# A two-attention transformer kernel: in the first attention the turn of a finished output moves behind the next tile's values, into the banks of the turned weights

## The chip, the core and the metric

The kernel runs on one core of a Trainium2 chip. The metric is device time in microseconds (us) from the start to the end of one launch. The core has five engines that run their own instruction lists in order and meet at semaphores: TensorE (PE in the rows; its weight loads are PEld), VectorE (DVE), ScalarE (ACT), GpSimd (POOL) and SyncE (SP), which issues most of the transfers. Matrix products and transposes land in PSUM, eight banks of 128 x 512 float32.

## The reference

Two transformer blocks run one after the other on 1024 tokens of width 1024. The change touches only the attention of the first one:

```python
def forgetting_attention(q, k, v, log_f):
    scale = 1.0 / math.sqrt(dh)
    c = jnp.cumsum(log_f, axis=1).transpose(0, 2, 1)
    ...
    def one_block(args):
        q_i, c_i, s0 = args
        scores = jnp.einsum('bqhd,bkhd->bhqk', q_i, k).astype(jnp.float32) * scale
        scores = scores + c_i[:, :, :, None] - c[:, :, None, :]
        ...
        scores = jnp.where(causal, scores, -jnp.inf)
        probs = jax.nn.softmax(scores, axis=-1).astype(v.dtype)
        return jnp.einsum('bhqk,bkhd->bqhd', probs, v)
```

There are 8 heads of width 64 and 8 blocks of 128 queries. Before it stand a norm and the projection, behind it the pooled branch, the output product and the gated feed-forward layer; the second block has two layers, the last of which holds a second attention (`diff_attention`, 6 heads of width 128).

## The kernel before

A class `Attention` serves both attentions; `diff` is true in the second one. The first handles its heads in four pairs (`n` = 4), one behind the other, and in each pair eight tiles of 128 queries (`iq` = 0 to 7), 32 tiles in all. A tile with index `iq` sees `iq` + 1 blocks of 128 keys, so "the five-block tile" below is `iq` = 4. Tile `t` goes through these steps (class, then the line of its main instruction):

- `Scores`: TensorE multiplies queries by keys into banks 0 to 3 (L1760); VectorE adds the bias and takes the maximum, once for each of the two heads (L1778, then L1781).
- `Exponentials`: ScalarE (L1791), once for each head. `Normalise`: VectorE takes the reciprocals of the sums (L1799, L1801).
- `Values`: the weights are turned on TensorE in groups of up to four blocks (L1827) into bank 4 + g % 2, where g is the running number of the group; each group is copied to SBUF and multiplied by the values (L1836) into the output's bank 6 + `iq` % 2. A tile of up to four blocks has two groups, one for each head; a larger one has four: four blocks and the rest of head 0, then the same of head 1.
- `ScaleOut`: VectorE divides the output by the sums (L1870). `TurnOut`: TensorE turns it (L1891), and ScalarE copies it away (L1898).

`Attention.steps` sets the order, which is the same for every engine. For tile t it is: `Normalise`(t), `ScaleOut`(t-1), `Scores`(t+1), `TurnOut`(t-1), all of `Values`(t), `Exponentials`(t+1). `fill` puts nothing in between in the first attention. Inside `Values` the list of TensorE is: turn group 1, turn group 2, multiply group 1, turn group 3, multiply group 2, and so on.

Who copies a turned group depends on its number alone:

```python
    def copied(self, g):
        return "pt_dve" if g % 2 and not self.diff else "pt_act"
```

An even g is copied by ScalarE (L1849), an odd one by VectorE (L1858). Every tile has an even count of groups, and g starts at zero, so group 1 of a tile is always even and ScalarE's. In VectorE's list the copies of tile t stand behind both bias passes of tile t+1. The turned output shares the bank of its own values (6 or 7, columns 128 to 255). `Prepare` and `Join` stand around the attention: no engine goes on before all are done.

Of the kernel before, what the change touches and what calls it, by code (L numbers as in the profile page):

```python
# [1636 lines left out]
class Attention:  # L1637
# [6 lines left out]
    def __init__(self, k, n, q, keys, v, out, sc, pt, on, nkeys, bias, diff=False, out_banks=2, ready=lambda i, iq: ()):  # L1644
        self.k, self.s, self.id = k, k.s, k.new_id()
        self.n, self.q, self.keys, self.v, self.out, self.nkeys, self.bias, self.diff = n, q, keys, v, out, nkeys, bias, diff
        self.out_banks, self.ready, self.waited = out_banks, ready, set()
        self.sc, self.pt, self.on = k.at(sc, 4, S), k.at(pt, 2, HALF), k.at(on, 2, P)
        self.heads = 1 if diff else 2
        self.per_pair = sum(self.of_tile(iq) for iq in range(ST))  # L1650
        self.outs = {self.out_group(i, iq) for i in range(n) for iq in range(ST)} if diff else set()

    def stat(self, iq, h):
        c = 4 * ((2 * iq + h) % 16)
# [5 lines left out]
    def steps(self, fill=lambda t, place: ()):  # L1660


        part = lambda kind, t, *more: [kind(self.k, self, *divmod(t, ST), *more)]
        last = self.n * ST - 1
        out = part(Scores, 0) + part(Exponentials, 0)
        for t in range(last + 1):
            out += part(Normalise, t)
            if t:
                out += part(ScaleOut, t - 1)
            if t < last:  # L1670
                out += part(Scores, t + 1)
            out += fill(t, 0)
            if t and not self.diff:
                out += part(TurnOut, t - 1)
            out += fill(t, 1)
            for n in range(len(self.groups(*divmod(t, ST))) + 1):
                out += part(Values, t, n)
                if n == 0:
                    out += fill(t, 2)
            if t < last:  # L1680
                out += part(Exponentials, t + 1)
            if t and self.diff:
                out += part(TurnOut, t - 1)
            out += fill(t, 3)
        return out + part(ScaleOut, last) + part(TurnOut, last)

    def groups(self, i, iq):


        g = i * self.per_pair + sum(self.of_tile(j) for j in range(iq))  # L1690
        if self.diff:
            g += max(i * ST + iq - 1, 0)
        nj, out = self.nkeys(iq) // P, []
        for h in range(self.heads):
            for first in range(0, nj, 4):
                out.append((g, h, first, min(4, nj - first)))
                g += 1
        return out
# [113 lines left out]
class Values(AttentionStep):  # L1812
# [7 lines left out]
    def pe(self, pe):  # L1820
        k, s, of, i, iq = self.k, self.s, self.of, self.i, self.iq
        for g, h, first, m in self.turned:
            if first == 0:
                pe.wait_ge(*s["combined" if of.diff else "exped"].at((of.id, i, iq, h)))
            k.bank_free(pe, 4 + g % 2)
            for j in range(m):
                ins = pe.transpose(k.ps[:, 4 + g % 2, j * P:(j + 1) * P], of.sc[:, of.buf(iq, h), (first + j) * P:(first + j + 1) * P], k.ident)  # L1827
            ins.then_inc(*s.turned_p.up((of.id, g)))
            k.free[4 + g % 2] = (of.copied(g), (of.id, g))
        for g, h, first, m in self.valued:  # L1830
            nj, b, o = of.nkeys(iq) // P, of.out_bank(iq), slice(0, P) if of.diff else slice(64 * h, 64 * h + 64)
            if first == 0 and h == 0:
                k.bank_free(pe, b)
            pe.wait_ge(*s[of.copied(g)].at((of.id, g)))
            for j in range(m):
                ins = pe.matmul(k.ps[:, b, o], of.pt[:, g % 2, j * P:(j + 1) * P], of.v(i, first + j)[:, o],  # L1836
                                start=(first + j == 0), stop=(first + j == nj - 1))
            ins.then_inc(*s.valued.up((of.id, g)))
            if of.diff:
                k.free[b] = ("scaled_out", (of.id, i, iq))  # L1840

    def act(self, act):
# [8 lines left out]
    def dve(self, dve):  # L1851
        k, s, of = self.k, self.s, self.of
        for g, h, first, m in self.turned:
            if of.copied(g) == "pt_dve":
                dve.wait_ge(*s.turned_p.at((of.id, g)))
                if g > 1:
                    dve.wait_ge(*s.valued.at((of.id, g - 2)))
                dve.tensor_copy(of.pt[:, g % 2, 0:m * P], k.ps[:, 4 + g % 2, 0:m * P]).then_inc(*s.pt_dve.up((of.id, g)))  # L1858


# [13 lines left out]
class TurnOut(AttentionStep):  # L1874


    def place(self):
        k, of = self.k, self.of
        if of.diff:
            b = 4 + of.out_group(self.i, self.iq) % 2  # L1880
            return b, k.ps[:, b, 0:P]
        b = of.out_bank(self.iq)
        return b, k.ps[:, b, P:2 * P]

    def pe(self, pe):
        k, s, of, i, iq = self.k, self.s, self.of, self.i, self.iq
        b, to = self.place()
        pe.wait_ge(*s.scaled_out.at((of.id, i, iq)))
        if of.diff:
            k.bank_free(pe, b)  # L1890
        pe.transpose(to, of.on[:, iq % 2, :], k.ident).then_inc(*s.turned_out.up((of.id, i, iq)))  # L1891
        k.free[b] = ("out_copied", (of.id, i, iq))

# [1431 lines left out]
```

## Time and profile before

| What | us |
|---|---|
| median of 3 runs | 3353.5 |
| the runs | 3343.42, 3353.5, 3353.6 |
| the profiled execution | 3344.59 |
| its span, first to last instruction | 3343.3 |
| TensorE busy in it | 2864.3 (86%) |
| VectorE, ScalarE, GpSimd busy | 1715.0, 986.0, 686.9 |
| first attention, first score to last copy | 254 to 442 |
| second attention | about 2865 to 3162 |

The profiled execution's time is its span and 1.3 us around it. It stands near the lowest of the three runs; the other two are 9 us above it. A busy share says little by itself here: TensorE has the largest one, but inside an attention tile it stops for the other engines several times, and what a change is worth is read from those stops. The column PEclk of the windows is the clock that TensorE was granted: 1.00 is 2.4 GHz and 0.50 is 1.2 GHz.

### The profile page before, as it was taken

The numbers are of one execution on the slowest core, as the hardware profiler recorded it, in microseconds if no ns is written. First come the engines' busy times: TensorE is split into PE (matmuls) and PEld (weight loads), VectorE is DVE, ScalarE is ACT, GpSimd is POOL, SyncE is SP. The second block draws the span as 40 slices with busy tenths as digits, with TensorE's granted clock in tenths as the row PEclk, the third lists the DMA queues.
The fourth block names the chain that finished last, engine by engine and source line by source line (L and its number), as shares of the span: only waits on it lengthen the run. The fifth ranks groups of instructions, "written<-read, shape, count | busy, mean of one in ns | idle before, by whom it ended". The sixth has DMA issues, their size and how long they took to land.

```text
span 3343.3 us, 49988 instructions
## 1 busy us (share of the span) xinstructions
PE 2864.3 (86%) x20746; PEld 2296.5 (69%) x20746; DVE 1715.0 (51%) x3034; ACT 986.0 (29%) x1803; POOL 686.9 (21%) x531
## 2 busy tenths in 40 slices
PE   7978878699999999689999867777748899999767
PEld 6765667588888888567888646666627678766545
DVE  3425555544444444666554157777654433377634
ACT  3224444311111111633221211111143222255543
POOL 2112233211011110262111012222212211122123
PEclk9988999899999999899999968998979899999978
DMA  3111032011111111113112100000032201111222
GB/s 105 45 51 39 14 100 65 26 58 50 45 51 51 45 51 50 39 57 94 45 38 64 55 1 3 3 3 3 3 113 76 92 29 44 34 33 35 79 82 76
DMA packets 196450, 162.46 MB, mean 49 GB/s; under 512 B 5200, under 2 KB 173818, under 8 KB 195458
## 3 DMA queue, kind: packets, MB, share of 16 engines
q1 hardware_dynamic: 196226, 159.26, 15.1%
q8 instruction: 167, 2.74, 0.3%
q14 instruction: 57, 0.47, 0.0%
HBM read 137.19 MB, written 22.05 MB: 48 GB/s over the span
## 4 chain that ended last, share of the span: by engine, by line
PE 70%; DVE 16%; ACT 6%; issue 4%; POOL 2%; DMA 2%; SPq 0%; POOLq 0%; DVEq 0%; ACTq 0%
PE ps L721 15%; PE ps L723 14%; PE ps L722 14%; PE ps L2267 5%; PE ps L1836 3%; PE ps L1760 3%; DVE r L686 2%; PE ps L1462 1%; PE ps L1464 1%; PE ps L1463 1%; PE ps L773 1%; ACT r L681 1%; PE ps L1827 1%; PE ps L775 1%; PE ps L774 1%
## 5 line engine op out<-in xcount | busy, mean ns | idle before, releaser
L721 PE MATMUL ps<-r,r 128*128 128x512 f32 (+1 forms) x2304 | 939.7, 408 | 145.5 <-DVE r L686 118.5
L722 PE MATMUL ps<-r,r 128*128 128x512 f32 (+1 forms) x2304 | 911.1, 395 | 0.0
L723 PE MATMUL ps<-r,r 128*128 128x512 f32 (+1 forms) x2304 | 910.6, 395 | 0.0
L721 PEld LDWEIGHTS ps<-r,r 128*128 128x128 f32 x2304 | 444.6, 193 | 280.7 <-DVE r L686 132.1
L667 POOL TENSOR_TENSOR sb<-sb 128x1024 f32<-128x1024 f32 x138 | 281.6, 2046 | 1350.7 <-DMA sb<-in_w_ffn_up 483.5
L722 PEld LDWEIGHTS ps<-r,r 128*128 128x128 f32 x2304 | 445.3, 193 | 93.2 <-issue 6.2
L723 PEld LDWEIGHTS ps<-r,r 128*128 128x128 f32 x2304 | 443.3, 192 | 94.9
L2267 PE MATMUL ps<-sb 64*64 64x64 f32 (+2 forms) x8832 | 299.6, 226 | 120.0 <-DVE sb L2515 31.4
L2267 PEld LDWEIGHTS ps<-sb 64*64 64x64 f32 (+1 forms) x8832 | 278.9, 135 | 150.4 <-issue 100.1
L686 DVE TENSOR_TENSOR r<-sb,r 128x1024 fp32r<-128x1024 f32 x198 | 273.9, 1391 | 190.9 <-ACT r L681 190.5
L681 ACT CAST r<-sb 128x1024 fp32r<-128x1024 f32 x198 | 204.9, 1043 | 229.0 <-POOL sb L667 228.9
L1836 PE MATMUL ps<-sb 128*128 128x64 f32 (+1 forms) x1008 | 144.2, 288 | 22.2 <-ACT sb L1849 17.2
L1836 PEld LDWEIGHTS ps<-sb 128*128 128x128 f32 x1008 | 131.3, 201 | 41.8 <-issue 20.9
L1462 PE MATMUL ps<-r,r 128*128 128x512 f32 x352 | 138.7, 394 | 8.1 <-DVE sb L1475 7.5
L926 DVE TENSOR_TENSOR sb<-sb 128x512 f32<-128x512 f32 x70 | 61.9, 885 | 163.2 <-ACT sb L916 151.7
L1414 ACT CAST r<-sb 128x512 fp32r<-128x512 f32 x44 | 27.3, 620 | 384.9 <-DVE sb L1429 384.9
L1463 PE MATMUL ps<-r,r 128*128 128x512 f32 x352 | 137.1, 389 | 0.0
L1464 PE MATMUL ps<-r,r 128*128 128x512 f32 x352 | 137.1, 389 | 0.0
L1778 DVE CUSTOM_DVE_ANT_0 sb<-ps,sb 128x128 f32<-128x128 f32 (+7 forms) x160 | 121.0, 756 | 28.0 <-PE ps L1760 20.5
L1475 DVE TENSOR_TENSOR sb<-sb,ps 128x512 f32<-128x512 f32 x160 | 105.9, 684 | 54.6 <-PE ps L1464 54.6
L1791 ACT ACTIVATE sb<-sb 128x128 f32<-128x128 f32 (+7 forms) x160 | 123.1, 772 | 26.3 <-DVE sb L1781 25.8
L1760 PE MATMUL ps<-sb 64*128 64x512 f32 (+2 forms) x480 | 103.6, 537 | 23.7 <-DVEq L298 16.1
(276 smaller groups left out, 3602.1 us busy)
## 6 DMA issues: line engine op xcount, KB each, us to landing
sb<-in_w_out SPq DMA_DIRECT2D x36, 512.0 KB, 4.0
sb<-in_a_w_in SPq DMA_DIRECT2D x29, 512.0 KB, 4.0
sb<-in_w_ffn_gate SPq DMA_DIRECT2D x22, 512.0 KB, 3.8
sb<-in_w_ffn_up SPq DMA_DIRECT2D x22, 512.0 KB, 3.8
sb<-in_w_ffn_down SPq DMA_DIRECT2D x22, 512.0 KB, 3.5
sb<-in_w_in SPq DMA_DIRECT2D x17, 512.0 KB, 4.0
sb<-in_x SPq DMA_DIRECT2D x16, 512.0 KB, 5.5
xs<-sb SPq DMA_DIRECT2D x4, 2048.0 KB, 9.7
```

Source lines behind the costliest of these rows:

```text
L667: pool.tensor_tensor(w.raw, w.raw, w.gain.unsqueeze(2).broadcast_to((P, w.nk, w.n)), ALU.mult).then_inc(*s.w_gain.up(w.id))
L681: act.copy(w.hi, w.raw).then_inc(*s.w_hi.up(w.id))
L686: dve.tensor_tensor(w.lo, w.raw, w.hi.bitcast(F32), ALU.subtract).then_inc(*s.w_lo.up(w.id))
L721: pe.matmul(self.out, w.hi[:, q, self.cols], hi, start=(q == 0), stop=False)
L722: pe.matmul(self.out, w.hi[:, q, self.cols], lo, start=False, stop=False)
L723: ins = pe.matmul(self.out, w.lo[:, q, self.cols], hi, start=False, stop=(q == w.nk - 1))
L1462: pe.matmul(self.out, w.hi[:, 0, cols], hi, start=(q == 0), stop=False)
L1463: pe.matmul(self.out, w.hi[:, 0, cols], lo, start=False, stop=False)
L1464: ins = pe.matmul(self.out, w.lo[:, 0, cols], hi, start=False, stop=(q == 1))
L1760: ins = pe.matmul(k.banks(2 * h)[:, b:b + m], of.q(i)[o, iq * P:(iq + 1) * P], of.keys(i)[o, b:b + m], start=True, stop=True)
L1836: ins = pe.matmul(k.ps[:, b, o], of.pt[:, g % 2, j * P:(j + 1) * P], of.v(i, first + j)[:, o], start=(first + j == 0), stop=(first + j == ...
L2267: ins = pe.matmul(self.bank(b + p // n, n, w)[o, p % n, :], lhs[o, p], rhs[o, p], start=(j == 0), stop=(j == len(pairs) - 1), skip_group_c ...
```

## The change

`TurnOut`(t-1) of the first attention moves behind all of `Values`(t) and `Exponentials`(t+1), where the second attention has had it. Its result now goes into bank 4 or 5, as if it were one more group of turned weights, so it takes a number g of its own, and all later groups move on by one.

```diff
-        self.outs = {self.out_group(i, iq) for i in range(n) for iq in range(ST)} if diff else set()
+        self.outs = {self.out_group(i, iq) for i in range(n) for iq in range(ST)}
...
             out += fill(t, 0)
-            if t and not self.diff:
-                out += part(TurnOut, t - 1)
             out += fill(t, 1)
...
             if t < last:
                 out += part(Exponentials, t + 1)
-            if t and self.diff:
+            if t:
                 out += part(TurnOut, t - 1)
...
-        if self.diff:
-            g += max(i * ST + iq - 1, 0)
+        g += max(i * ST + iq - 1, 0)
...
-            if of.diff:
+            if (g, h, first, m) == self.g[-1]:
                 k.free[b] = ("scaled_out", (of.id, i, iq))
...
-                if g > 1:
-                    dve.wait_ge(*s.valued.at((of.id, g - 2)))
+                if of.pt_before(g) >= 0:
+                    dve.wait_ge(*s.valued.at((of.id, of.pt_before(g))))
...
     def place(self):
-        k, of = self.k, self.of
-        if of.diff:
-            b = 4 + of.out_group(self.i, self.iq) % 2
-            return b, k.ps[:, b, 0:P]
-        b = of.out_bank(self.iq)
-        return b, k.ps[:, b, P:2 * P]
+        b = 4 + self.of.out_group(self.i, self.iq) % 2
+        return b, self.k.ps[:, b, 0:P]
...
         pe.wait_ge(*s.scaled_out.at((of.id, i, iq)))
-        if of.diff:
-            k.bank_free(pe, b)
+        k.bank_free(pe, b)
```

`copied` is unchanged. The file is three lines shorter above the touched classes, so L1760 becomes L1757, L1827 becomes L1824, L1836 becomes L1833, L1858 becomes L1855, L1778 becomes L1775, and L1891 becomes L1883.

TensorE's list at the five-block tile of the second pair: behind the next tile's scores (L1760) stands the turned output, then the turned groups and the products. A row ends in the semaphores that its instruction waits for; `s_pt_act` and `s_pt_dve` are ScalarE's and VectorE's copies of turned weights. Before:

```order
L1760 MATMUL ps<-sb 128x256 x2
L1891 MATMUL ps<-sb 128x128 [waits s_scaled_out]
L1827 MATMUL ps<-sb 128x128 [waits s_pt_act,s_exped]
L1827 MATMUL ps<-sb 128x128 x3
L1827 MATMUL ps<-sb 128x128 [waits s_pt_dve]
L1836 MATMUL ps<-sb 128x64 [waits s_pt_act,s_out_copied]
L1836 MATMUL ps<-sb 128x64 x3
L1827 MATMUL ps<-sb 128x128 [waits s_pt_act,s_exped]
L1827 MATMUL ps<-sb 128x128 x3
L1836 MATMUL ps<-sb 128x64 [waits s_pt_dve]
```

Now:

```order
L1757 MATMUL ps<-sb 128x256 x2
L1824 MATMUL ps<-sb 128x128 [waits s_pt_dve,s_exped]
L1824 MATMUL ps<-sb 128x128 x3
L1824 MATMUL ps<-sb 128x128 [waits s_out_copied]
L1833 MATMUL ps<-sb 128x64 [waits s_pt_dve,s_scaled_out]
L1833 MATMUL ps<-sb 128x64 x3
L1824 MATMUL ps<-sb 128x128 [waits s_pt_dve,s_exped]
L1824 MATMUL ps<-sb 128x128 x3
L1833 MATMUL ps<-sb 128x64 [waits s_pt_act]
```

The turned output has left this place (it stands behind the tile's last product as L1883), and the product of group 1 now waits for VectorE's copy, that of group 2 for ScalarE's.

VectorE's list at the same tile, from the first bias pass of the next tile (768 keys; ISA is the fused add and maximum) to the copies. Before:

```order
L1778 ISA sb<-ps,sb 128x768 [waits s_turned_p,s_bias_made,s_scored]
L1778 ISA sb 128x1
L1781 TENSOR_SCALAR sb<-sb 128x1 [waits s_biased]
L1858 COPY sb<-ps 128x128 [waits s_valued,s_turned_p] x2
L1799 RECIPROCAL sb<-sb 128x1 [waits s_exped]
```

Now:

```order
L1775 ISA sb<-ps,sb 128x768 [waits s_turned_p,s_bias_made,s_scored]
L1775 ISA sb 128x1
L1778 TENSOR_SCALAR sb<-sb 128x1 [waits s_biased]
L1855 COPY sb<-ps 128x512 [waits s_valued,s_turned_p] x2
L1796 RECIPROCAL sb<-sb 128x1 [waits s_exped]
```

VectorE's two copies have grown from 128 to 512 columns, and ScalarE has the two of 128 instead. The place of the copies in the list is the same. It is so in the tiles of one, three, five and seven blocks (but for the very first tile), since one number goes to an output per tile and the numbers of every second tile become odd where they were even; the tiles of two, four, six and eight blocks keep their copies. The lists of GpSimd and SyncE, and everything outside the first attention, are the same.

## Rows read from the trace of the kernel before

**Rows 1.** windows, first attention; us, busy of PE, PEld, DVE, ACT, POOL, PEclk, DMA

```profile
260.48:278.06 17.58, 17.28 (x60) 11.09 (x61) 8.28 (x37) 6.03 (x21) 5.06 (x8) 0.50 0.00 1
278.06:442.12 164.06, 143.72 (x1026) 111.00 (x1024) 94.16 (x327) 77.33 (x186) 35.82 (x52) 1.00 0.05 20
260.48:309.83 49.35, 45.67 (x272) 33.97 (x272) 25.74 (x93) 21.20 (x55) 11.38 (x18) 0.82 0.06 22
356.20:399.98 43.78, 38.46 (x274) 29.43 (x273) 25.72 (x92) 20.98 (x53) 10.63 (x16) 1.00 0.06 25
```

**Rows 2.** timeline, five-block tile, third pair; start, length, engine, line, [idle before]

```profile
369.06 1.56 PE L1760 MATMUL ps<-sb 64*128 64x512 f32 x8
...
370.71 0.71 PE L1827 MATMUL ps<-sb 128*128 128x128 f32 x5
...
372.08 1.08 PE L1836 MATMUL ps<-sb 128*128 128x64 f32 x8 [0.66 <-ACT sb L1849]
...
372.88 0.29 DVE L1858 COPY sb<-ps 128x128 f32<-128x128 f32 x1
...
372.99 0.61 PE L1827 MATMUL ps<-sb 128*128 128x128 f32 x4
...
374.28 1.33 PE L1836 MATMUL ps<-sb 128*128 128x64 f32 x10 [0.39 <-ACT sb L1849]
...
375.53 1.77 PE L1760 MATMUL ps<-sb 64*128 64x512 f32 x8
```

**Rows 3.** timeline, seven-block tile, third pair

```profile
382.45 1.99 PE L1760 MATMUL ps<-sb 64*128 64x512 f32 x8
...
384.53 0.93 PE L1827 MATMUL ps<-sb 128*128 128x128 f32 x7
...
387.23 0.56 DVE L1858 COPY sb<-ps 128x384 f32<-128x384 f32 x1
...
388.89 1.70 PE L1836 MATMUL ps<-sb 128*128 128x64 f32 x14
...
390.52 0.49 PE L1760 MATMUL ps<-sb 64*128 64x128 f32 x4
```

**Rows 4.** timeline, three-block tile, third pair

```profile
362.51 0.56 DVE L1858 COPY sb<-ps 128x384 f32<-128x384 f32 x1
...
363.12 0.88 PE L1836 MATMUL ps<-sb 128*128 128x64 f32 x6 [0.24 <-DVE sb L1858]
...
363.93 1.35 PE L1760 MATMUL ps<-sb 64*128 64x512 f32 x8
```

**Rows 5.** groups of instructions by form, 254 to 482 us; busy, mean ns | idle before

```profile
L1898 ACT COPY sb<-ps 128x128 f32<-128x128 f32 x32 | 8.5, 266 | 65.6 <-PE ps L1891 65.6
...
L1858 DVE COPY sb<-ps 128x512 f32<-128x512 f32 x12 | 8.3, 692 | 12.3 <-PE ps L1827 12.3
...
L1891 PEld LDWEIGHTS ps<-sb 128*128 128x128 f32 x32 | 4.6, 143 | 17.5 <-DVE sb L1870 14.1 <-issue 3.1
```

**Rows 6.** windows, second attention: six stops of TensorE and the 3.0 us after each

```profile
2935.44:2940.96 5.52, 2.67 (x23) 2.46 (x23) 4.42 (x12) 3.17 (x9) 3.75 (x2) 1.00 0.00 0
2979.35:2984.87 5.52, 3.00 (x14) 2.72 (x14) 4.25 (x11) 2.96 (x9) 3.99 (x3) 0.69 0.15 45
3025.77:3031.29 5.52, 2.72 (x15) 2.47 (x16) 4.41 (x12) 3.17 (x9) 3.74 (x2) 0.81 0.00 0
3071.04:3076.56 5.52, 3.00 (x14) 2.72 (x14) 4.25 (x11) 2.95 (x9) 3.99 (x3) 0.73 0.14 43
3113.54:3118.84 5.30, 2.67 (x22) 2.46 (x23) 3.98 (x14) 2.47 (x9) 0.00 (x0) 1.00 0.00 0
3154.20:3159.93 5.73, 2.68 (x19) 2.47 (x19) 1.93 (x4) 2.12 (x5) 0.00 (x0) 0.91 0.02 4
```

**Rows 7.** timeline, TensorE alone, first pair

```profile
268.72 2.08 PE L1760 MATMUL ps<-sb 64*128 64x512 f32 x4
...
275.23 2.51 PE L1760 MATMUL ps<-sb 64*128 64x512 f32 x8
```

## The prediction

> **What bounds the kernel now.** The change lives in the first attention, so I read the windows of that stretch first [rows 1]. From 278 us on TensorE is granted the full clock, 2.4 GHz (1.00), and is busy for 143.72 of 164.06 us; a pair of heads takes 43.78 us there and repeats to the hundredth. TensorE is the bound, with stops. In the first 17.58 us it runs at 1.2 GHz (0.50), and the first pair takes 49.35 us for the same work. Then the timeline of single tiles shows what ends the stops. At the five-block tile [rows 2] TensorE does the next tile's scores from 369.06, turns groups 1 and 2 from 370.71, and multiplies group 1 at 372.08, as soon as ScalarE has copied it. VectorE, meanwhile, does the two bias passes of the next tile; only at 372.88 is it free for its copy of group 2, and TensorE is then still busy with group 1. So the slow copier sits where it is covered: behind a group that ScalarE delivers early. The three-block tile shows the same end without enough cover: VectorE copies at 362.51, and TensorE has waited 0.24 us when it multiplies at 363.12 [rows 4].
>
> **Part 1, the turn leaves its place.** Its weight load waits 17.5 us in all, most of it for the scaling on VectorE, and ScalarE's 32 copies of it (266 ns each, 8.5 us) stand ahead of the first copy of turned weights [rows 5]. That wait is gone: groups 1 and 2 are turned earlier by the turn's own share of the list, between 0.11 us (the step from one transpose to the next) and 0.28 (one alone) [rows 2]; I take 0.16. But nearly nothing follows, since the next wait in the tile is for VectorE's copy, which stands behind the bias passes, and those start at the end of the scores, which has not moved. I count the gain at 0, between 0 and the 0.16 us of each of 31 tiles, 5 us.
>
> **Part 2, the turn in its new place.** It stands between the tile's last product and the next scores, where TensorE has no stop to hide it. It costs the 0.11 us between one transpose and the next (0.61 us for 4, of which the last alone is 0.28: [rows 2]); 31 of them are 3.4 us. Its own waits are met: the scaling was done at the start of the tile, its bank's copy too. Its copy on ScalarE now stands behind the next tile's exponentials, and group 2 of that tile waits for it. Only in the eight-block tile, where the exponentials of 1024 keys are late, may that be seen: 0 to 0.56 us (the length of the 384-column copy in [rows 3]), and I take 0.1.
>
> **Part 3, who copies.** This is the main term. The output takes one number per tile, so in the tiles of one, three, five and seven blocks group 1 becomes VectorE's. Its copy stands in VectorE's list behind both bias passes of the next tile. TensorE has nothing else in its list before the product of group 1, so it now stops until VectorE is free.
>
> Five blocks [rows 2]. The copy starts at 372.88 as before, but is 512 columns long, 0.69 us [rows 5], so group 1 is multiplied at 373.62 instead of 372.08 (0.05 us from the copy's end to the product). Group 3's turn comes 0.91 us later, as it does now (372.08 to 372.99), at 374.53, and is done at 375.14; VectorE copies it until 375.86; groups 3 and 4 are multiplied from 375.91. Today that is 374.28, so the tile loses 1.63, and with the turn 1.74 us.
>
> Seven blocks [rows 3]. The copy starts at 387.23 and ends at 387.92; group 1 is multiplied at 387.97. From there 0.91 to group 3's turn, 0.72 and 0.45 for the rest of group 2's work and group 4's turn, 0.33 more: groups 3 and 4 start at about 390.4 instead of 388.89. The loss is 1.5, with the turn 1.6 us.
>
> Three blocks [rows 4]. Group 1 is multiplied at 363.12, where group 2 is now, and group 2 behind it. The loss is one group, 0.73, with the turn 0.84 us. One block: the same with a group of one, 0.24, with the turn 0.35 us.
>
> The other four tiles of a pair lose the turn alone, and one of them the 0.1: 0.11 x 4 + 0.1 = 0.54. A pair loses 1.74 + 1.6 + 0.84 + 0.35 + 0.54 = 5.1 us. The first pair has an unchanged first tile and runs its three-block tile at half clock, where slower TensorE hides a part (0.6 for 0.84): 4.5 us; the last tile of all has no next tile: 0.2 less. **Sum: 4.5 + 3 x 5.1 - 0.2 = 19.6 us.** The end of the attention is a join of all engines, so nothing behind it can take this back.
>
> **Part 4, the clock.** In the five-block tile TensorE is now idle from about 371.26 (the turns' end, 371.42, less 0.16) to 373.62: 2.36 us. In the seven-block tile it is idle from 385.30 (384.53 + 0.93 less 0.16) to 387.97: 2.67 us. Today the longest stop in these tiles is 0.66 us [rows 2], and the clock holds at 1.00 throughout [rows 1]. How does it take stops of this size? The trace has six of 2.3 to 2.7 us in the second attention, each with transposes and small products around it [rows 6]; a window there is the stop and 3.0 us behind it, so the first stop is 5.52 - 3.0 = 2.52 us. In four of the six windows PEclk is below 1.00, so the clock fell to 1.2 GHz. I take 4 in 6 for each stop here. The Trainium skill ("TensorE: Matmul & The Clock Gate", section on a second failure mode, cycling of the PSUM queue) says that even micro-idles between groups of matmuls make the clock swing. By that the kernel of before would swing too, with its stops of 0.2 to 0.7 us in each tile, and it does not; rows 6 bear the rule out only for the long ones.
>
> What a fall costs hangs on how long it lasts. In the first pair the clock stayed at 0.50 through the tiles of one, two and three blocks, though TensorE was busy 17.28 of 17.58 us, past the 2.08 us of scores at 268.72, and rose only with the larger scores at 275.23 [rows 1, 7]. So turned and multiplied groups of 64 columns do not bring it back; eight matmuls of scores do. A fall in the five-block tile meets the next large scores soon: some 2.6 us of work is left in the tile and takes twice as long, 2.5 lost, and the scores (1.77 us in rows 2) lose 1 more, 3.5 us. A fall in the seven-block tile finds no large scores until four tiles later. It costs about 3 in the rest of that tile, 4.7 in the eight-block tile (32 products and 16 transposes at the 0.12 and 0.11 us each of rows 3 are 5.6 us, and most of that doubles), and then what the first pair lost in the same tiles, 49.35 - 43.78 = 5.6 less 0.5 for stops that a slow TensorE hides: 3 + 4.7 + 5.1 = 12.8 us. In the last pair there is only 3 + 4.7 = 7.7. **Sum: 0.67 x (4 x 3.5 + 3 x 12.8 + 7.7) = 40 us**; 0 if none falls, 60 if all eight do.
>
> **Total.** 3344.6 (the profiled execution: span 3343.3 and 1.3 around it) + 19.6 + 40 = 3404 us. The median of the runs is 3353.5, 9 us above that execution, since two of three stood there; against it the same sum is 3353.5 + 60 = **3413 us**, and that is my figure.
>
> **The rivals.**
> Only the stops, no falls: the clock forgives stops of 2.4 and 2.7 us. For it: two of the six windows of rows 6 stayed at 1.00. Against it: eight such stops must all, or nearly all, get by. It gives 3353.5 + 20 = 3373, with one or two falls 3385.
> Nothing measurable: VectorE is free before ScalarE would be. It would be so if the bias passes ended before group 1 is turned; they end 1.5 us later in rows 2, and only in the two smallest tiles is it close. It gives 3350 to 3360.
> Faster: the wait for the scaled output was what held the tile up, and VectorE's new copies run beside it. The Trainium skill ("Perfetto Trace Analysis", section Matmuls) says that independent groups should rotate through PSUM banks so that their copies overlap the next group's matmuls, and the output now rotates with the groups. By rows: the 17.5 us of waiting and part of the 8.5 us of ScalarE's copies [rows 5] would come back, 3353.5 - 21 = 3332. It decides if TensorE reaches group 1's product later than VectorE's copy ends; in rows 2 it is there 1.5 us earlier. Nearly excluded.
>
> **How the numbers follow.** Three or more falls, 3385 to 3435: 0.66. Stops with at most two falls, 3366 to 3385: 0.25. Nothing: 0.05. Faster: 0.04. A measurement here tells about 0.3%, 10 us, from no change. So slower by over 0.3% is 0.66 + 0.25 = 0.91, within it 0.05, faster 0.04. The range leaves out the last two and the far ends of the others: the low end is the stops alone, 3366, and the high end all eight falls, 3353.5 + 79.6 = 3433, with a little for their price, 3438.
>
> **What would show it.** In the profile after, the first product of the five-block tile waits for VectorE's copy for over 2 us, and the idle time ahead of the values' line is some 40 us more, with VectorE's copy as its releaser. VectorE's 512-column copies go from 12 to 28, ScalarE's from 36 to 20. A warm pair without a fall takes 48.9 us instead of 43.78. PEclk in the slices of the first attention drops below 1.00 behind the seven-block tiles and stays low for over 15 us. Wrong would be: ScalarE still first in those tiles; a pair of under 46 us (the bias passes are not in the way); a clock at 1.00 over all four pairs (part 4 falls, 3373); or a fall that mends itself within 4 us after the seven-block tile (its price is then a third, and the time about 3385).

## The result: 1.9% slower, and the profile after

The changed kernel takes 3411.78 us in the median of six runs (3403.36 to 3416.21), the kernel before 3349.14 us in six (3343.42 to 3353.60). The ratio is 1.0187, with a 95% interval of 1.0171 to 1.0203, or 62.6 us more. The forecast was 3413 us.

The profiled execution of the changed kernel has a span of 3411.1 us, 67.8 more than before. The windows of its first attention follow: length, busy time of PE, PEld, DVE, ACT and POOL, PEclk, share and rate of the transfers. The first row is the whole attention, the others are five stretches at half clock in it.

```profile
253.79:504.99 251.20, 210.76 (x1088) 160.71 (x1088) 108.22 (x368) 79.60 (x208) 42.25 (x64) 0.71 0.05 17
287.88:294.71 6.83, 6.83 (x25) 4.10 (x23) 2.20 (x8) 2.00 (x6) 0.21 (x1) 0.50 0.21 86
304.94:335.66 30.72, 29.44 (x125) 23.66 (x124) 10.58 (x44) 8.73 (x26) 4.46 (x7) 0.50 0.01 1
366.38:407.34 40.96, 38.24 (x159) 30.75 (x160) 14.85 (x58) 12.15 (x35) 6.88 (x11) 0.50 0.00 0
434.65:438.06 3.41, 3.41 (x20) 3.41 (x18) 0.69 (x1) 0.13 (x1) 0.00 (x0) 0.50 0.00 0
489.26:499.50 10.24, 10.10 (x48) 9.85 (x49) 2.15 (x6) 3.60 (x7) 0.00 (x0) 0.50 0.01 2
```

The attention is 251.20 us long. Before it was 188.15 us, from the first score at 254.27 to the end of the last copy at 442.42, so 63.05 of the 67.8 us are here. TensorE's mean clock has gone down to 0.71 of full, and the stretches are long ones: the third and the fourth row, 30.7 and 41.0 us, answer to a clock of 1.00 from 278 to 442 us in [rows 1]. On the page the same shows in the 40 slices of the clock, in tenths, where the fourth to the sixth slice are the attention:

```profile
PEclk9986689989999999989999968999988899999978
```

The five-block tile of the second pair answers to [rows 2]. The timeline, with the idle time before an instruction in brackets:

```profile
343.29 1.56 PE L1757 MATMUL ps<-sb 64*128 64x512 f32 x8
...
344.78 0.77 PE L1824 MATMUL ps<-sb 128*128 128x128 f32 x5
...
347.11 0.69 DVE L1855 COPY sb<-ps 128x512 f32<-128x512 f32 x1
...
347.95 1.08 PE L1833 MATMUL ps<-sb 128*128 128x64 f32 x8 [2.40 <-DVE sb L1855]
...
348.86 0.63 PE L1824 MATMUL ps<-sb 128*128 128x128 f32 x4
...
350.27 2.40 PE L1833 MATMUL ps<-sb 128*128 128x64 f32 x10 [0.24 <-DVE sb L1855]
```

The scores start at 343.29, the groups are turned at 344.78, and then TensorE stands for 2.40 us. VectorE starts its copy, now of 512 columns, at 347.11, behind the bias passes, and group 1 is multiplied at 347.95. Behind the stop the clock is low (it fell at 349.32): the ten products of the last row, 1.33 us in rows 2, take 2.40 us.

The seven-block tile, TensorE alone, answers to [rows 3]:

```profile
361.39 1.99 PE L1757 MATMUL ps<-sb 64*128 64x512 f32 x8
363.31 0.98 PE L1824 MATMUL ps<-sb 128*128 128x128 f32 x7
367.01 1.94 PE L1833 MATMUL ps<-sb 128*128 128x64 f32 x8 [2.71 <-DVE sb L1855]
...
371.40 3.09 PE L1833 MATMUL ps<-sb 128*128 128x64 f32 x14
...
374.64 0.80 PE L1757 MATMUL ps<-sb 64*128 64x128 f32 x4
```

The stop is 2.71 us, and 13.25 us pass between the two rows of scores, where rows 3 have 8.07.

The groups of instructions by form from 253 to 540 us (busy, mean ns of one | idle before and who ended it) answer to [rows 5]:

```profile
L1833 PE MATMUL ps<-sb 128*128 128x64 f32 x576 | 103.4, 341 | 34.2 <-DVE sb L1855 30.6 <-ACT sb L1846 2.8
...
L1855 DVE COPY sb<-ps 128x512 f32<-128x512 f32 x28 | 19.4, 692 | 36.0 <-PE ps L1824 36.0
...
L1846 ACT COPY sb<-ps 128x512 f32<-128x512 f32 x20 | 11.7, 586 | 46.7 <-PE ps L1824 46.7
...
L1883 PEld LDWEIGHTS ps<-sb 128*128 128x128 f32 x32 | 8.4, 261 | 0.6 <-DVE sb L1867 0.6
```

VectorE's copies of 512 columns went from 12 to 28 and ScalarE's from 36 to 20. The weight load of the output's turn waits 0.6 us instead of 17.5, so the wait that the change removes is gone. What took its place is the first row: the products waited 34.2 us, 30.6 of it for VectorE's copies. Two groups of the same view of the kernel before, for these two lines:

```profile
L1836 PE MATMUL ps<-sb 128*128 128x64 f32 x576 | 81.4, 283 | 18.8 <-ACT sb L1849 14.0 <-DVE sb L1858 4.4
...
L1849 ACT COPY sb<-ps 128x512 f32<-128x512 f32 x36 | 21.1, 585 | 30.7 <-PE ps L1827 30.7
```

The products then waited 18.8 us, 4.4 of it for VectorE. They were also busy for 81.4 us instead of 103.4: the same 576 instructions, 283 ns each instead of 341.

### The profile page after: what moved, and what is told of

Read it like the earlier page. It is cut to its first block, busy times and chain, and to the rows that moved or that the text cites. A ratio compares the mean times of both kernels' runs of the same rounds, so it can differ in the third digit from the quotient of the medians.

```text
span 3411.1 us, 50020 instructions
## 1 busy us (share of the span) xinstructions
PE 2917.9 (86%) x20746; PEld 2337.9 (69%) x20746; DVE 1721.0 (50%) x3034; ACT 982.1 (29%) x1803; POOL 691.4 (20%) x531
## 3 DMA queue, kind: packets, MB, share of 16 engines
q8 instruction: 166, 2.72, 0.3%
## 4 chain that ended last, share of the span: by engine, by line
PE 70%; DVE 16%; ACT 5%; issue 4%; POOL 2%; DMA 2%; SPq 0%; POOLq 0%; DVEq 0%; ACTq 0%
PE ps L721 15%; PE ps L722 14%; PE ps L723 14%; PE ps L2259 5%; PE ps L1833 4%; PE ps L1757 3%; PE ps L1824 2%; DVE r L686 2%; PE ps L1462 1%; PE ps L1463 1%; PE ps L1464 1%; PE ps L773 1%; ACT r L681 1%; PE ps L775 1%; DVE sb L1775 1%
## 5 line engine op out<-in xcount | busy, mean ns | idle before, releaser
L2259 PE MATMUL ps<-sb 64*64 64x64 f32 (+2 forms) x8832 | 301.3, 226 | 121.5 <-DVE sb L2507 28.9
L1833 PE MATMUL ps<-sb 128*128 128x64 f32 (+1 forms) x1008 | 162.2, 316 | 37.6 <-DVE sb L1855 30.6
L1833 PEld LDWEIGHTS ps<-sb 128*128 128x128 f32 x1008 | 151.5, 229 | 56.5 <-issue 48.3
L1775 DVE CUSTOM_DVE_ANT_0 sb<-ps,sb 128x128 f32<-128x128 f32 (+7 forms) x160 | 121.0, 757 | 47.7 <-PE ps L1757 40.7
L1414 ACT CAST r<-sb 128x512 fp32r<-128x512 f32 x44 | 27.3, 620 | 384.9 <-DVE sb L1429 384.9
L1757 PE MATMUL ps<-sb 64*128 64x512 f32 (+2 forms) x480 | 116.2, 594 | 23.3 <-DVEq L298 15.9
```

Of the source, the lines that this page charges most:

```text
L1757: ins = pe.matmul(k.banks(2 * h)[:, b:b + m], of.q(i)[o, iq * P:(iq + 1) * P], of.keys(i)[o, b:b + m], start=True, stop=True)
L2259: ins = pe.matmul(self.bank(b + p // n, n, w)[o, p % n, :], lhs[o, p], rhs[o, p], start=(j == 0), stop=(j == len(pairs) - 1), skip_group_c ...
```

## The experiments

Each of these kernels computes the whole reference. The time of a tile runs from the start of the scores that are issued in it to the start of the next ones, so it is read from rows like those above. The kernels of one group ran on one chip, and each is read against the runs of before beside it. Those had a median of 3344.4 us (19 runs) for the first four kernels (copier by place, swap without the change, kept busy, ScalarE as the only copier) and 3342.5 us (14 runs) for the next four. The three second traces are one launch each, on another chip, where before took 3342.11 us.

The times of the tiles of one pair, in us, are put together here, so that each experiment can be read against them. The rows marked "full clock" are pairs in which the clock stayed at 1.00; the other rows are single pairs with falls.

| Blocks of the tile | 1 | 2 | 3 | 4 | 5 | 6 | 7 | 8 | sum |
|---|---|---|---|---|---|---|---|---|---|
| before, full clock | 2.61 | 3.44 | 4.28 | 5.12 | 6.48 | 6.91 | 8.07 | 6.85 | 43.76 |
| the change, pair with falls | 4.09 | 4.91 | 6.08 | 5.24 | 9.52 | 8.58 | 13.25 | 11.31 | 62.98 |
| the change kept busy, full clock | 3.01 | 3.56 | 5.07 | 5.24 | 8.27 | 6.99 | 9.68 | 6.87 | 48.69 |
| copier by place, full clock | 2.72 | 3.56 | 4.40 | 5.24 | 6.49 | 7.00 | 8.19 | 6.58 | 44.18 |
| ScalarE copies all, new place | 2.08 | 2.96 | 3.84 | 4.72 | 6.49 | 6.92 | 7.37 | 6.64 | 41.02 |
| ScalarE copies all, old place | 3.31 | 4.91 | 5.24 | 4.71 | 6.48 | 6.91 | 7.36 | 12.12 | 51.04 |

### The change without the swap: the copier by place

The theory was that the place of the turn costs next to nothing, and that the swapped copiers are the loss. The edit asks for the place of a group in its tile instead of its number:

```diff
-        return "pt_dve" if g % 2 and not self.diff else "pt_act"
+        if self.diff:
+            return "pt_act"
+        for i in range(self.n):
+            for iq in range(ST):
+                for n, group in enumerate(self.groups(i, iq)):
+                    if group[0] == g:
+                        return "pt_dve" if n % 2 else "pt_act"
```

> The change, but the copier goes by the place of a group in its tile (first and third ScalarE, second and fourth VectorE) and no longer by its running number, so every tile keeps the copiers of before; the turn of the output stays in its new place and bank. Theory (the swapped copiers and the clock they put down are the whole cost): the time of before plus the 31 turns in TensorE's list at 0.11 us, less a little: 3346 to 3358 us, no stop of TensorE over 0.7 us in these tiles, clock 1.00 from the first pair's four-block tile to the end of the attention. Rival (the place itself costs: the bank shared with the weights, the output's copy behind the exponentials): 3365 us or more, with the second group's turn waiting for the output's copy.

It took 3353.75 us in the median of ten runs (3342.3 to 3358.89), 1.0021 of before (1.0007 to 1.0035). The loss of 1.87% is 0.21% without the swap. At full clock a pair takes 44.18 us, 0.42 more than before: 0.09 to 0.12 us in each of six tiles, 0.01 in the five-block tile, less 0.27 in the eight-block tile. No stop in these tiles is over 0.7 us. But one part of the theory fell. The windows of its attention, the whole and one stretch:

```profile
253.90:449.88 195.98, 170.34 (x1088) 128.08 (x1088) 103.37 (x368) 84.03 (x208) 42.25 (x64) 0.89 0.06 22
342.60:369.90 27.30, 26.90 (x112) 20.96 (x111) 10.21 (x43) 8.37 (x26) 4.38 (x7) 0.50 0.00 1
```

The clock was not at 1.00 to the end. It fell once for 27.3 us, at the seven-block tile, where no long stop stands. The timeline of TensorE there, in two pieces:

```profile
336.48 1.99 PE L1763 MATMUL ps<-sb 64*128 64x512 f32 x8
...
339.83 1.07 PE L1839 MATMUL ps<-sb 128*128 128x64 f32 x8 [0.44 <-ACT sb L1852]
```

```profile
341.87 0.94 PE L1839 MATMUL ps<-sb 128*128 128x64 f32 x6 [0.53 <-DVE sb L1861]
...
343.25 3.09 PE L1839 MATMUL ps<-sb 128*128 128x64 f32 x14
```

The stops are 0.44 and 0.53 us, the same as in the tiles at which it did not fall. A second launch of the same kernel was traced to see whether that belongs to the program:

> The copier by place once more, for a second trace. Theory (the fall of 27.3 us at the second seven-block tile was met by chance): the attention without it, 184 to 190 us long, or with one at another tile. Rival (the turn's new place brings it there each time): a fall at the second seven-block tile again, the attention about 196 us long.

```profile
253.45:442.74 189.29, 161.49 (x1088) 120.39 (x1088) 103.35 (x368) 84.63 (x208) 42.40 (x64) 0.94 0.06 23
290.90:442.74 151.84, 132.18 (x948) 101.36 (x948) 86.32 (x301) 71.79 (x174) 31.69 (x47) 1.00 0.04 15
```

It does not. This launch took 3351.85 us. There the clock is at 1.00 from 290.9 us to the end and the attention takes 189.29 us instead of 195.98. But it has a fall of its own, of 6.8 us, at the five-block tile of the first pair:

```profile
284.13:290.96 6.83, 6.62 (x24) 3.89 (x23) 2.42 (x8) 2.23 (x6) 0.29 (x1) 0.50 0.42 154
```

The stops ahead of it are 0.66 and 0.39 us. So each of the two launches had one fall behind short stops, at different tiles. This kernel and the one before are at half clock about equally long then (23.9 us here, 23.8 before), which leaves some 1.1 us of the attention to the turn's new place. Whether the new place makes these short-stop falls more frequent than before is not settled by two traces.

Nor is all of the 0.21%, some 7 us, in the attention. From its end to the end of the launch every kernel here runs the same program, and the thirteen profiled executions take 2898.1 to 2911.8 us for it: 2900.9 before, 2906.3 and 2907.8 in the two traces of this kernel, 2906.1 in the change. Differences of the whole time of less than some 10 us between single launches say little about the attention.

### The swap without the change

The other half of the same question: before.py with nothing moved, but the copiers swapped in the same tiles.

```diff
+                        return "pt_dve" if (n + (iq % 2 == 0 and i + iq > 0)) % 2 else "pt_act"
```

> The kernel before, with nothing moved, but VectorE and ScalarE swapped as copiers in the same tiles as in the change (one, three, five and seven blocks, but for the very first tile). Theory: nearly the whole loss is there without the change: 3395 to 3412 us, the 3.4 us of turns missing, stops of 2.2 to 2.7 us ahead of the first product in the tiles of five and seven blocks, and the clock falling behind them. Rival (the turn's place matters as well): clearly under 3385 us.

It took 3413.18 us (3408.83 to 3420.07, four runs), 1.0207 of before (1.0185 to 1.0229): the whole loss, and none of the change. The window of its attention, and the first product of a five-block tile:

```profile
254.34:512.67 258.33, 218.32 (x1088) 170.40 (x1088) 108.91 (x368) 79.79 (x208) 42.26 (x64) 0.68 0.05 17
```

```profile
352.62 1.94 PE L1842 MATMUL ps<-sb 128*128 128x64 f32 x8 [2.29 <-DVE sb L1864]
```

The stop is 2.29 us, where the change has 2.40, and the turn of the output uses the difference. The time stands just above the 3412 us that the theory allowed; the clock was down longer in the traced launch (0.68 of full in the mean) than in that of the change (0.71). All eight long stops of this trace, 2.28 to 2.61 us, have a fall in them or behind them.

### The stops with TensorE kept busy

To part the stops from the clock, transposes of the identity fill the stops of the changed kernel. They go to columns of the output's bank that nothing reads:

```diff
             if first == 0 and h == 0:
                 k.bank_free(pe, b)
+                if not of.diff and i + iq > 0 and iq in (2, 4, 6):
+                    for _ in range({2: 10, 4: 17, 6: 20}[iq]):
+                        pe.transpose(k.ps[:, b, 2 * P:3 * P], k.ident, k.ident)
```

> The change, with transposes of the identity into unused columns of the output's bank put ahead of the first product of the tiles of three (10), five (17) and seven blocks (20), at 0.11 us each, so that TensorE works through most of the stop that VectorE's copy leaves; nothing reads them. Theory (of the 63 us that the attention is longer, about 20 are stops and 43 are the half clock): the clock stays at 1.00 from the first pair on, the first products start when they did, and the time is 3365 to 3377 us. Rival (the waits alone make the loss and the clock costs little): 3400 us or more. Rival (the clock falls for the small products, not for the stops): it falls here too.

It took 3365.20 us (3362.73 to 3371.83, four runs), 1.0059 of before (1.0037 to 1.0081). Its attention, and from 279 us on:

```profile
254.18:461.80 207.62, 183.69 (x1276) 142.74 (x1276) 107.80 (x368) 79.55 (x208) 42.42 (x64) 0.93 0.06 21
279.00:461.80 182.80, 165.24 (x1187) 130.42 (x1186) 96.37 (x319) 70.84 (x182) 34.09 (x50) 0.96 0.05 18
```

A five-block tile, TensorE alone:

```profile
330.06 1.56 PE L1757 MATMUL ps<-sb 64*128 64x512 f32 x8
...
332.15 2.02 PE L1833 MATMUL ps<-sb 128*128 128x128 f32 x17
334.63 1.10 PE L1836 MATMUL ps<-sb 128*128 128x64 f32 x8 [0.46 <-DVE sb L1858]
...
336.96 1.33 PE L1836 MATMUL ps<-sb 128*128 128x64 f32 x10 [0.50 <-DVE sb L1858]
...
338.33 1.77 PE L1757 MATMUL ps<-sb 64*128 64x512 f32 x8
```

The 17 transposes of the second row stand in the stop, and 0.46 us of it are left. VectorE still sets the start of group 1's product, at 334.63, 4.57 us behind the scores, and the tile still takes 338.33 - 330.06 = 8.27 us. But the ten products of group 3 and 4 take 1.33 us again, as in rows 2, and the long falls are gone; two of 6.8 us are left in the profiled execution, both behind stops of 1.26 us in the one-block tile, which I had not filled (the third such stop has none). The theory had the clock at 1.00 throughout, so that part was missed; the time lies at the lower end of what it allowed.

So of the 63 us of the attention, 207.62 - 188.15 = 19.5 are left when most stops are filled, and 251.20 - 207.62 = 43.6 are the clock. The 19.5 are not stops alone. The two short falls cost 1.6 us each (the second pair takes 50.29 us where the third takes 48.69). Against that, the clock rose at 271.2 us in the first pair instead of 278.1, worth some 2.4 us: the three- and four-block tiles there take 6.51 and 6.28 us before, 3.4 over full clock, and 6.02 and 5.24 here, 1.0 over it. The stops alone are 19.5 - 3.2 + 2.4 = 18.7 us by this estimate, and the rest of the 63, some 44, is the clock.

### One kind of tile at a time

Two kernels with the copier by place, and the swap in one kind of tile alone:

```diff
+                        return "pt_dve" if (n + (iq == 4)) % 2 else "pt_act"
```

and `iq == 6` in the other.

> The copier by place, but with VectorE and ScalarE swapped in the tiles of five blocks alone (4 of 32 tiles). Theory (a fall of the clock there meets large scores soon and is short): a stop of 2.4 us in each of the four tiles, the tile 1.6 us longer at full clock, a fall behind most of them that lasts 3 to 10 us and costs 2 to 3.5: 12 to 20 us over the copier by place without swaps, 1.005 to 1.008 of before. Rival (every stop costs the same): half of what seven blocks cost or more.

> The same with the swap in the tiles of seven blocks alone. Theory (no large scores follow until the four-block tile of the next pair, so the clock stays down for about 30 us): a stop of 2.7 us, 1.6 us each at full clock, and 10 to 13 us for each fall but the last: 30 to 45 us over the copier by place, 1.010 to 1.015 of before, more than twice the swap in the five-block tiles. Rival (every stop costs the same): 12 to 20 us, as there.

The swap at five blocks gave 3368.50 us (3365.01 to 3371.17, four runs), 1.0075 (1.0060 to 1.0090). The swap at seven gave 3376.90 us (3368.28 to 3386.56, four runs), 1.0109 (1.0089 to 1.0128). Against the copier by place (1.0021) these are 18 us and 29 us, each for four stops; the second is just short of the 30 to 45 us of the theory, and 1.6 times the first instead of more than twice. The attention with the swap at five blocks and two of its four falls:

```profile
254.46:464.54 210.08, 177.23 (x1088) 132.00 (x1088) 106.55 (x368) 82.35 (x208) 42.41 (x64) 0.86 0.06 21
287.20:297.40 10.20, 9.66 (x37) 6.64 (x36) 3.19 (x9) 2.96 (x7) 0.29 (x1) 0.50 0.26 103
338.40:345.20 6.80, 6.30 (x21) 3.98 (x22) 1.62 (x6) 2.38 (x6) 0.00 (x0) 0.50 0.33 135
```

With the swap at seven blocks, and three of its four:

```profile
254.40:464.03 209.63, 177.10 (x1088) 136.89 (x1088) 104.62 (x368) 83.23 (x208) 42.26 (x64) 0.86 0.06 21
300.80:311.00 10.20, 10.02 (x48) 9.51 (x48) 2.43 (x12) 3.52 (x7) 0.99 (x2) 0.50 0.01 2
352.00:365.70 13.70, 13.70 (x68) 12.97 (x66) 3.26 (x13) 4.96 (x12) 0.99 (x2) 0.50 0.00 1
403.20:406.60 3.40, 3.40 (x19) 3.40 (x19) 0.69 (x1) 0.23 (x1) 0.00 (x0) 0.50 0.00 0
```

Each of the eight stops put the clock down. But the falls at the seven-block tile lasted 10.2, 13.7, 3.4 and 6.8 us here, not about 30, and the two traced attentions are equally long, 210.08 and 209.63 us. That the swap at seven blocks costs more shows in the medians alone, of four launches that span 18 us. A second trace of that kernel and one of the changed kernel show how much of this belongs to the launch:

> The swap in the seven-block tiles alone once more, for a second trace. Theory (as above): other lengths of the four falls than 10.2, 13.7, 3.4 and 6.8 us, one or more of 20 us or over, since this kernel's launches span 18 us. Rival: the same lengths.

> The changed kernel once more, for a second trace. Theory (whether a stop of 2.4 or 2.7 us puts the clock down, and for how long it stays down, hangs on where the launch meets the clock's own rhythm): the stops are the same to 0.1 us, the falls begin at other places of the tiles and the four falls at the seven-block tiles have other lengths than 30.7, 41.0, 3.4 and 10.2 us; the attention is 235 to 260 us long. Rival (the lengths belong to the program): the same four lengths in the same order.

The swap at seven blocks, traced again (3375.45 us), had falls of 3.4, 13.7, 3.4 and 20.5 us; of 20 us and over there is one, the last, which runs past the end of the attention, and two of the four had kept their length. The changed kernel, traced again (3417.45 us), with its attention and the stretch behind the third pair's seven-block tile:

```profile
254.21:512.44 258.23, 218.72 (x1088) 167.06 (x1088) 108.56 (x368) 79.59 (x208) 42.39 (x64) 0.68 0.05 17
435.10:465.80 30.70, 29.34 (x124) 23.56 (x123) 10.63 (x45) 8.82 (x26) 4.50 (x8) 0.50 0.00 1
```

All eight long stops are there again, 2.40, 2.71 or 2.72 us each, and each has a fall in it or within 2.6 us behind it. Six of the eight falls begin within 0.2 us of the same place in their tile, where the theory had them at other places. The first two falls at seven blocks last as long as in the first trace (30.7 and 41.0 us) and so does the last (10.2); the third lasts 30.7 instead of 3.4 us. Mostly by that fall the attention is 258.23 us long instead of 251.20. So neither side has it whole: the program sets the stops, and which length a fall has repeats in most places and changes in some. What is shown is that the falls behind long stops are the program's, 16 of 16, while their lengths are partly the launch's, or the chip's.

### ScalarE as the only copier

If VectorE's copy behind the bias passes is what ends the stops, then no copy should stand there at all:

```diff
-        return "pt_dve" if g % 2 and not self.diff else "pt_act"
+        return "pt_act"
```

This was run twice on the changed kernel, and once on the kernel before, whose turn stands in the old place.

> The change with ScalarE as the copier of all groups of turned weights, as in the second attention. Theory (what ends a tile's stops is a copy that stands in VectorE's list behind the bias passes of the next tile): now no copy stands there, so the stops go in all tiles, the unchanged ones too: 5 to 15 us less than the copier by place gives, 3335 to 3348 us. Rival (ScalarE becomes the bound: 21 of 43.8 us busy in a pair before, and about 8 more, with the exponentials behind the copies): 3355 us or more, waits of VectorE's reciprocals for the exponentials.

> The change with ScalarE as the copier of all groups once more, beside the kernel with the old place, on the same chip and for a tighter interval. Theory: 0.997 to 0.999 of before, the attention about 178 us long. Rival (the earlier 0.9977 was the chance of the clock elsewhere in the program): 1.000 or more.

> The kernel before, with the turn of the output in its old place, and ScalarE as the copier of all groups. It tells what the new place is worth once the copier is out of the way. Theory (the old place makes TensorE wait for the scaled output, and ScalarE copies the output ahead of group 1, some 0.3 us in each tile that nothing hides any more): the attention 4 to 10 us longer than with the new place and ScalarE as the copier (177.94 us), 0.998 to 1.001 of before. Rival (the place is worth nothing): within 1 us of 177.94, 0.9977 of before.

With the new place it took 3337.15 us (3328.65 to 3343.38, ten runs), 0.9977 of before (0.9963 to 0.9991), and the second time 3335.84 us (3329.27 to 3342.67, nine runs), 0.9979 (0.9969 to 0.9990). Both times lie in the range of the theory, and it is faster than both kernels: 7 us below before in the medians. The attention of the second of these, whole and from 278 us:

```profile
252.38:427.86 175.48, 154.53 (x1088) 117.50 (x1088) 83.78 (x320) 98.85 (x256) 42.26 (x64) 0.95 0.07 25
278.00:427.86 149.86, 134.99 (x993) 104.65 (x991) 72.96 (x272) 88.74 (x225) 33.95 (x50) 1.00 0.07 22
```

It is 175.48 us long, 12.7 less than before, at a clock of 1.00 from 278 us on; the first trace has 177.94. Part of the 12.7 is the first pair's clock, low for 17.0 us here and for 23.8 before. At full clock a pair is 2.74 us shorter: the tiles of one to four blocks are 0.4 to 0.5 us shorter each, the seven-block tile 0.7, the eight-block tile 0.2, and those of five and six are as before. VectorE's copies are short there (128 and 256 columns) and, as rows 2 show for five blocks, were covered.

With the old place, though, the same edit gave 3368.21 us (3363.01 to 3379.78, six runs), 1.0078 (1.0065 to 1.0092), where I had expected 0.998 to 1.001. Its attention and one fall, then the start of an eight-block tile:

```profile
252.96:466.74 213.78, 188.07 (x1088) 145.70 (x1088) 84.11 (x320) 100.53 (x256) 42.25 (x64) 0.78 0.06 21
303.10:323.60 20.50, 19.94 (x81) 15.27 (x80) 6.09 (x28) 7.16 (x24) 3.26 (x6) 0.50 0.00 0
```

```profile
300.16 1.14 ACT L1791 ACTIVATE sb<-sb 128x1024 f32<-128x1024 f32 x1
...
301.62 0.47 DVE L1870 TENSOR_SCALAR sb<-ps,sb 128x64 f32<-128x64 f32 x2
...
302.15 0.33 PE L1891 MATMUL ps<-sb 128*128 128x128 f32 x1 [1.61 <-DVE sb L1870]
```

ScalarE has four groups to copy in the seven-block tile before it comes to the exponentials of the eight-block tile. They end late, at 301.3, 1.25 us behind the start of the tile's scores, where the kernel before has them done 0.30 us ahead of it. VectorE's reciprocals and then its scaling of the output wait for them, and the turned output, which in the old place stands ahead of everything else of the tile, waits for the scaling: 1.61 us of stop in three pairs and 2.04 in the last. The clock fell there in each of the four pairs, for 20.5, 20.5, 20.5 and 13.7 us (the last runs past the end of the attention), and the eight-block tile takes 12.12 us. In the new place the turn is not needed until the products are done, and the same tile takes 6.64 us at full clock. This is what the new place is worth: nothing, or a loss of 0.2%, while ScalarE has half of the copies, and a gain of about 1% when it has all of them.

## Why the prediction was right, step by step

The figure was 3413 and the median is 3411.78. The rise against the median was put at 60 us and is 62.6. That the figure itself is off by 1.2 us only is luck: the 3353.5 that it was added to, the median of three runs, stands 4.4 us above the median of six, and the rise was put 3 us too low. The mechanism and its two parts hold, 19.6 forecast for the stops and 19.5 measured (18.7 for the stops alone), 40 forecast and 43.6 measured for the clock. Inside the second part two errors cancel, and that is luck too.

**The turn leaves its place (0).** Held. Its wait went from 17.5 to 0.6 us and brought next to nothing: with the copier by place a pair is 0.42 us longer, not shorter.

**The turn in its new place (0.11 us a tile, and 0.1 for the eight-block tile).** Held for six tiles (0.09 to 0.12 with the copier by place). The gain of part 1, which I had put at zero everywhere, exists in two tiles of that kernel, whose first product waits for ScalarE. At five blocks it starts 2.92 us behind the scores instead of 3.02, which pays for the turn. At eight blocks it starts 1.84 us behind them instead of 2.23, since the groups no longer wait for the scaled output, and the tile is 0.27 shorter. In the change itself the eight-block tile is 0.02 longer (kept busy, 6.87) and not 0.2. There the forecast wait of group 2 for the output's copy, behind the late exponentials, does show:

```profile
405.05 0.66 PE L1824 MATMUL ps<-sb 128*128 128x128 f32 x4 [0.26 <-ACT sb L1893]
```

**Who copies.** Held to a tenth of a microsecond, with the change kept busy as the measure: five blocks 1.79 (1.74 forecast), seven 1.61 (1.6), three 0.79 (0.84), one 0.40 (0.35), a pair 48.69 (48.9 in the list of what would show it). The stops are 2.40 and 2.71 us (2.36 and 2.67). That the swap alone makes the loss, and that its removal takes all but 0.21% of it away, is shown by the two experiments from either side.

**How many falls.** Mis-sized. I took 4 of 6 from [rows 6], and 16 of 16 long stops in two traces of the change put the clock down, 12 of 12 in three traces with the swap in one kind of tile, 8 of 8 with the swap in the kernel before. Rows 6 gave too low a chance. The stops there are as long, but the work around them is another; why two of those six left the clock up was not tried. The chances did not follow from the step either: with 4 in 6 for each of eight stops, taken as independent, three or more falls come out at 0.98, not 0.66.

**What a fall costs.** The step "turned and multiplied groups of 64 columns do not bring it back; eight matmuls of scores do" failed. The fall at 434.65 in the changed kernel ended at 438.06, in the middle of such products, before any scores. Nor did eight matmuls of scores always bring it back: in the fall from 366.38 to 407.34 the eight at 402.38 ran through at half clock, 2.51 us, and the clock rose some 2.4 us behind them. And in the first pair it rose at 270.81, behind the four at 268.15, the same four that were not enough in rows 7. At five blocks the price was right: against the kept-busy tiles the four falls cost 3.0, 2.8, 4.0 and 4.4 us in the tiles of five and six blocks (3.5 forecast). At seven blocks it was too high: 11.0, 14.2 and 1.6 us for 12.8, and 3.7 for 7.7. Together that is some 45 us for eight falls where the forecast had 60 for eight and took two thirds of them. (The change has two more falls of 3.4 us, behind stops of 1.33 and 1.62 us in three-block tiles. They cost 2.0 us, and the kept-busy kernel lost 3.2 to its own two: 44.7 + 2.0 - 3.2 = 43.5, the 43.6 measured.) The sum came out right because the chance was too low and the price too high. A reader should take the terms of this step less seriously than its sum.

**The rivals.** The one without falls gave 3373, and 3365 was measured (beside a before of 3344) when TensorE was kept busy, so its mechanism was priced right, but it is not what happens. The rule that groups should rotate through banks (the Trainium skill, "Perfetto Trace Analysis", section Matmuls) did not decide here: the output did rotate and the loss came from who empties the bank and when. Where the copies were all ScalarE's, the rotating place was the better one, by 1%, but through the wait for the scaling that it leaves, and not shown to be through the overlap that the rule speaks of.

**What I had said would show it.** The counts of the copies came as said. One item was wrong: the idle time ahead of the values' line rose by 15.4 us, not by 40. I had counted the loss of the clock into it, but a slow TensorE is busy, not idle; that part is in the busy time of the line, 22 us more. Of the clock, both what I had said would show it and what I had said would be wrong came: behind the seven-block tiles it stayed low for over 15 us in two pairs of four (30.7 and 41.0), and in the third pair it was back after 3.4 us.

What stays open is why a fall lasts 3 us in one place and 41 in another, and whether the place of the turn matters for the falls behind short stops.

## What to carry to other kernels

A counter that names a buffer by its parity may also choose the engine that serves it: whoever adds one number to such a sequence must list which engine does what afterwards, item by item. Then ask of each item what stands ahead of it in that engine's list; a copy that is cheap behind a covered group costs its whole wait ahead of the first one. And price a stop of TensorE twice, as idle time and as what the clock does behind it; here the second, some 44 us, was more than double the first, some 19.

## What the runs showed of the hardware

All 16 long stops in the two traces of the changed kernel, 2.40 to 2.72 us among transposes and 64-column products, had half clock in them or within 2.6 us behind them, and it lasted 3.4 to 41.0 us. Counted over the attention in all thirteen traces, from a full clock: 41 of 41 stops of 1.61 to 2.72 us did it (three of 1.61 and one of 2.04 in the kernel with the turn in the old place and ScalarE as the copier), and 6 of 11 stops of 0.96 to 1.55 us. And in each of the two launches of the copier by place the clock fell once with no stop over 0.7 us near: for 27.3 us behind stops of 0.44 and 0.53 us, and for 6.8 us behind stops of 0.66 and 0.39 us. The Trainium skill ("TensorE: Matmul & The Clock Gate", the section on cycling of the PSUM queue) says that micro-idles between groups of matmuls make the clock swing. I had held against it that the kernel before keeps 1.00 through 164 us of such stops; these two falls show that a fall behind short stops does come, though rarely. That it comes by the page's mechanism is not shown. Work that computes nothing, 0.11 us transposes of the identity, held the clock up (no fall began at any of the twelve stops that they filled) and took the loss from 1.87% to 0.59%, some 43 us.
